# Products that nobody reads, put in front of TensorE's waits in a two-block transformer kernel

## What is computed

```python
def first_block(x, ...):                       # x: 1 x 256 x 1024
    for l in range(DEPTH):                     # DEPTH = 2
        x = x + 0.5 * swiglu_ffn(rms_norm(x, ffn1_norm[l]), ffn1_w_in[l], ffn1_w_out[l])
        h = rms_norm(x, mix_norm[l])
        uv, c_q, c_kv, k_rope, z, xbc, dt_raw, gates = jnp.split(h @ w_in[l], IN_OFFSETS, axis=-1)
        y_a, y_b, y_c = gmlp_mixer(...), mla_mixer(...), ssd_mixer(...)
        g = jax.nn.sigmoid(gates).reshape(bsz, s, 3, 1024)
        merged = (g[:, :, 0] * (y_a @ w_branch[l, 0]) + g[:, :, 1] * (y_b @ w_branch[l, 1])
                  + g[:, :, 2] * (y_c @ w_branch[l, 2]))
        x = x + merged @ w_out[l]
        x = x + 0.5 * swiglu_ffn(rms_norm(x, ffn2_norm[l]), ffn2_w_in[l], ffn2_w_out[l])
    return x

def second_block(x, mem, ...):                 # one layer
    h = x + _mixer(_rmsnorm(x, norm_mix_g), ...)          # gated delta rule and S5
    h = h + _cross_attn(_rmsnorm(h, norm_x_g), mem, ...)
    h = h + _swiglu(_rmsnorm(h, norm_ffn_g), w_gate, w_up, w_down)
    return _rmsnorm(h, norm_final_g)
```

## Time and profile before

| | |
|---|---|
| median of three runs | 1987.09 us |
| the three runs | 1983.67, 1988.60, 1987.09 us |
| the profiled execution, device time | 1975.48 us |
| its span, first to last instruction | 1973.8 us |
| mean clock granted to TensorE in it | 0.976 of full |
| PE busy | 1875.1 us, 95% of the span |

### The profile page before, as it was taken

How to read it: one execution, slowest core, us unless ns; L and a number is a source line. 1 busy time by engine, 2 the same in 40 slices (tenths; PEclk the granted TensorE clock), 3 DMA queues, 4 the chain that set the end, 5 groups by cost and what they waited for, 6 DMA issues and landing times.

```text
span 1973.8 us, 25367 instructions
## 1 busy us (share of the span) xinstructions
PE 1875.1 (95%) x10644; PEld 1535.2 (78%) x10644; DVE 934.4 (47%) x1166; ACT 709.9 (36%) x813; POOL 77.9 (4%) x145
## 2 busy tenths in 40 slices
PE   7999999997999999999999978999899999889998
PEld 7998575576899789985755667998787975749996
DVE  4544134467555444441335574545667431234453
ACT  5543213143454345441131343554223121214542
POOL 0000000000000000000000002000361100000000
PEclk9999999998999989999999999999998899989999
DMA  6545434343653565454344437736344223326353
GB/s 235 173 140 191 150 119 152 128 134 106 208 171 128 192 212 172 141 192 140 130 132 133 134 117 121 240 120 212 131 150 115 65 78 131 112 85 213 128 180 129
DMA packets 192244, 293.02 MB, mean 148 GB/s; under 512 B 7218, under 2 KB 126804, under 8 KB 192164
## 3 DMA queue, kind: packets, MB, share of 16 engines
q1 hardware_dynamic: 189908, 287.72, 43.4%
q0 software_dynamic: 1936, 4.14, 2.0%
q10 hardware_dynamic: 320, 0.01, 0.0%
HBM read 289.49 MB, written 2.36 MB: 148 GB/s over the span
## 4 chain that ended last, share of the span: by engine, by line
PE 90%; DVE 4%; DMA 2%; ACT 2%; issue 1%; DVEq 0%; SPq 0%; ACTq 0%
PE acc L221 17%; PE acc L223 17%; PE acc L222 17%; PE acc L189 16%; PE acc L253 7%; PE acc L409 2%; PE acc L2374 1%; PE acc L203 1%; PE acc L2682 1%; PE turn L308 1%; DMA ring<-in_ffn_w_out 1%; DMA ring<-in_ffn_w_in 1%; DVE w_lo L381 1%; PE acc L1161 1%; ACT w_hi L377 1%
## 5 line engine op out<-in xcount | busy, mean ns | idle before, releaser
L381 DVE TENSOR_TENSOR w_lo<-ring,w_hi 128x2048 fp32r<-128x2048 f32 x160 | 362.9, 2290 | 273.1 <-ACT w_hi L377 272.6
L221 PE MATMUL acc<-xT_hi,w_hi 128*128 128x256 f32 x1680 | 477.1, 284 | 3.0 <-DVE w_lo L381 3.0
L223 PE MATMUL acc<-xT_hi,w_lo 128*128 128x256 f32 x1680 | 476.2, 283 | 2.4 <-issue 2.4
L222 PE MATMUL acc<-xT_lo,w_hi 128*128 128x256 f32 x1680 | 476.1, 283 | 0.0
L377 ACT ACTIVATE w_hi<-ring 128x2048 fp32r<-128x2048 f32 x160 | 302.1, 1913 | 221.2 <-DMA ring<-in_ffn_w_out 110.3
L221 PEld LDWEIGHTS acc<-xT_hi,w_hi 128*128 128x128 f32 x1680 | 323.3, 192 | 5.9 <-issue 5.8
L222 PEld LDWEIGHTS acc<-xT_lo,w_hi 128*128 128x128 f32 x1680 | 323.2, 192 | 0.1
L223 PEld LDWEIGHTS acc<-xT_hi,w_lo 128*128 128x128 f32 x1680 | 323.2, 192 | 0.0
L189 PE MATMUL acc<-ring,xT 128*128 128x512 f32 (+2 forms) x736 | 303.2, 571 | 0.8 <-DVE xT L2662 0.8
L189 PEld LDWEIGHTS acc<-ring,xT 128*128 128x128 f32 x736 | 140.2, 192 | 153.9 <-issue 141.3
L221 PE MATMUL acc<-w_hi,hT_hi 128*128 128x512 f32 x440 | 173.0, 393 | 4.7 <-DVE w_lo L381 4.7
(11 more groups left out here) (503 smaller groups left out, 1984.2 us busy)
## 6 DMA issues: line engine op xcount, KB each, us to landing
ring<-in_ffn_w_in SPq DMA_DIRECT2D x88, 1024.0 KB, 5.5
ring<-in_w_in SPq DMA_DIRECT2D x48, 1024.0 KB, 5.1
ring<-in_ffn_w_out SPq DMA_DIRECT2D x44, 1024.0 KB, 4.9
ring<-in_w_branch SPq DMA_DIRECT2D x12, 1024.0 KB, 5.0
ring<-in_w_out SPq DMA_DIRECT2D x12, 1024.0 KB, 5.0
ring<-in_w_gate SPq DMA_DIRECT2D x11, 1024.0 KB, 5.2
ring<-in_w_up SPq DMA_DIRECT2D x11, 1024.0 KB, 7.1
ring<-in_w_down SPq DMA_DIRECT2D x11, 1024.0 KB, 4.9
```

What stands on the lines that cost most here:

```text
L221: pe.matmul(o, a_hi, wh, start=start, stop=False)
L222: pe.matmul(o, a_hi, wl, start=False, stop=False)
L223: return pe.matmul(o, a_lo, wh, start=False, stop=stop)
L381: vec.tensor_tensor(w_part(w_lo, r), raw_part(c0, r), w_part(w_hi, r).bitcast(F32), ALU.subtract).then_inc(f.lo, 1)
```

## The change

A new helper `keep_busy(pe, o, n)` issues n products of the identity with `causal`, 256 columns in float32, into the accumulator `o`. Each starts anew in the accumulator, counts no semaphore and waits for none, and nothing reads its result; the next real product into the accumulator starts anew as well. 127 of them are issued, in 24 places: 18 at the program's beginning, 7 or 5 in front of each turning of a norm that has a wait, 4 in front of each `first_gate`, and in both mixers of the first block 5 behind `G_KV`, 2 in front of the values, 6 in front of the last branch, 5 in front of the merged turning and 6 in front of `w_out`; in cross attention 5 and 2. In two places a wait is moved or added so that the accumulator is free: `wait_acc_free` stands ahead of the 4 products of `first_gate`, and `qs_pv_pe` first waits for `qs.vec` at 50 rather than 52.

```diff
--- before.py
+++ after.py
@@ -300,7 +300,13 @@
                                       gain.unsqueeze(2).broadcast_to([P, KD, P])[:, 4 * hf:4 * hf + 4, :],
                                       ALU.mult).then_inc(s.vec, 1)
 
-        def norm_pe(pe, s, nb=xn, tiles=(0, 1)):
+        def keep_busy(pe, o, n):
+
+            for _ in range(n):
+                pe.matmul(o[:, 0:TOK], ident[:, :], causal[:, :], start=True, stop=True)
+
+        def norm_pe(pe, s, nb=xn, tiles=(0, 1), busy=0):
+            keep_busy(pe, turn[2 * tiles[0]], busy)
             for b in range(2 * tiles[0], 2 * tiles[-1] + 2):
                 m, hf = b // 2, b % 2
                 pe.wait_ge(s.vec, s.tile(m))
@@ -401,9 +407,10 @@
             def first_gate():
 
 
+                wait_acc_free(pe, G0, 0)
+                keep_busy(pe, acc[bank(G0, 0)], 4)
                 pe.wait_ge(n.vec, n.v0 + 8)
                 wait_chunk(pe, c0)
-                wait_acc_free(pe, G0, 0)
                 for ft in range(2):
                     for k in range(KD):
                         ins = pe.matmul(acc[bank(G0, 0)][:, ft * TOK:(ft + 1) * TOK],
@@ -1304,6 +1311,8 @@
                     vec.tensor_copy(dst, turn[r % 4][:, :].rearrange("p (h n) -> p h n", h=4)).then_inc(qs.vec, 1)
 
             def qs_pv_pe(pe):
+                pe.wait_ge(qs.vec, 50)
+                keep_busy(pe, turn[2], 2)
                 pe.wait_ge(qs.vec, 52)
                 for m in range(MT):
                     for h in range(H):
@@ -1329,6 +1338,8 @@
 
             def branch_pe(pe, j):
                 b = BRANCHES[j]
+                if j == 2:
+                    keep_busy(pe, turn[0], 6)
                 pe.wait_ge(tail.vec, 2 + j)
                 for n in range(2):
                     split_group_pe(pe, tail, G_BR + 2 * j + n, C_BR + 2 * j + n, 2 + 2 * j + n, yT_hi[:, b], yT_lo[:, b],
@@ -1357,6 +1368,7 @@
                         vec.tensor_tensor(dst, dst, br_t[:, n, m, :], ALU.add).then_inc(br.vec, 1)
 
             def merged_pe(pe):
+                keep_busy(pe, turn[0], 5)
                 pe.wait_ge(br.vec, 8)
                 for b in range(4):
                     m, hf = b // 2, b % 2
@@ -1426,6 +1438,7 @@
                 group_pe(pe, G_CQ, C_CQ, xT, (4, 4), QR)
                 gm_mix_pe(pe)
                 group_pe(pe, G_KV, C_KV, xT, (4, 4), KVR + ROPE)
+                keep_busy(pe, turn[2], 5)
                 turned_group_pe(pe, G_XBC0, C_XBC0, xT, 4, 512)
                 cq_pe(pe)
                 gm_turn_pe(pe)
@@ -1454,6 +1467,8 @@
                 qs_pv_pe(pe)
                 branch_pe(pe, 2)
                 merged_pe(pe)
+                wait_acc_free(pe, G_WO, 0)
+                keep_busy(pe, acc[bank(G_WO, 0)], 6)
                 pe.wait_ge(tail.vec, 8)
                 for n in range(2):
                     split_group_pe(pe, tail, G_WO + n, C_WO + 2 * n, 8 + 2 * n, xT_hi, xT_rest, part_hi, part_lo, 2,
@@ -1566,12 +1581,12 @@
                 add_norm_vec(vec, ffn_add(C_FFN2, G_FFN2, 0.5, 3 * l + 3), n_next, gain0[:, 8 * l + 8:8 * l + 16])
 
             def pe_program(pe):
-                norm_pe(pe, n1, tiles=(1,) if l > 0 else (0, 1))
+                norm_pe(pe, n1, tiles=(1,) if l > 0 else (0, 1), busy=7 if l > 0 else 18)
                 if l == 0:
                     first_gain_pe(pe)
                 ffn_pe(pe, f1, n1, C_FFN1, G_FFN1, lambda e: norm_pe(e, mix_norm, tiles=(0,)), asides={7: params_pe})
                 mixer_pe(pe)
-                norm_pe(pe, n2)
+                norm_pe(pe, n2, busy=5)
                 ffn_pe(pe, f2, n2, C_FFN2, G_FFN2, lambda e: norm_pe(e, n_next, tiles=(0,)), asides={4: params2_pe, 6: s5_c_pe} if l == DEPTH - 1 else {})
 
             def sync_program(sync):
@@ -2707,7 +2722,7 @@
                 for product, which in itertools.islice(beside, n):
                     product(pe, *which)
 
-            norm_pe(pe, nm, tiles=(1,))
+            norm_pe(pe, nm, tiles=(1,), busy=7)
             pe.wait_ge(nm.vec, nm.v0 + NORM_DONE)
             turned_group_pe(pe, G_K2, C_K2, xT, 4, 512)
             turned_group_pe(pe, G_Q2, C_Q2, xT, 4, 512)
@@ -2741,17 +2756,19 @@
             pe.wait_ge(rc.vec, RC_DONE)
             group_pe(pe, G_WO2, C_WO2, xT, (4, 4), 512)
             group_pe(pe, G_WO2 + 1, C_WO2 + 2, xT, (4, 4), 512, for_x=True)
-            norm_pe(pe, nx)
+            norm_pe(pe, nx, busy=5)
             pe.wait_ge(nx.vec, nx.v0 + NORM_DONE)
             turned_group_pe(pe, G_XQ, C_XQ, xT, 4, 512)
             turned_group_pe(pe, G_XQ + 1, C_XQ + 2, xT, 4, 512)
             xa_scores_pe(pe)
+            keep_busy(pe, acc[0], 5)
             xa_turn_pe(pe)
+            keep_busy(pe, acc[0], 2)
             xa_pv_pe(pe)
             pe.wait_ge(xa.vec, 18)
             group_pe(pe, G_XO, C_XO, xT, (4, 4), 512)
             group_pe(pe, G_XO + 1, C_XO + 2, xT, (4, 4), 512, for_x=True)
-            norm_pe(pe, n3)
+            norm_pe(pe, n3, busy=5)
             ffn_pe(pe, f3, n3, C_FFN3, G_FFN3, lambda e: None)
 
         def second_act(act):
```

## The result

The changed kernel takes **1964.09 us** (median of four runs, 1960.97 to 1966.40); the kernel before took 1986.19 beside it. The ratio is 0.9888, 95% interval 0.9867 to 0.9909: faster by 22 us, 1.1%. The forecast was 1960 in a range of 1950 to 1975.

A forecast was written before the change was run, and what follows sets the result against it. PE bounds the kernel, with 90% of the chain and half clock behind its waits. Terms -18.0 + 2.1 + 0.1 + 0.5 = -15.3 us, from the profiled 1975.48, gave 1960 us; range 1950 to 1975.

The forecast's parts named there:

- The mechanism: At PE's waits: new products keep PE busy, so the clock does not fall there; 18.0 us taken away.
- `w_out`: Stretches at `w_out` in two layers: half-clock loss taken away, 2.8 us in the first and 1.5 in the second.
- `n1`: Norm `n1` of the second layer: 2.9 us of clock loss and 0.7 of slow turning taken away, first gate 0.79 late.
- the attention: Attention: 1.7 us of clock loss at the values and 0.7 of slow turning taken away, 0.1 of cost.
- Late first gates: 4 products before each first gate outlast the wait: 0.43 us at `n2` (twice) and `n3`, 0.79 at `n1`, together 2.1.
- The beginning: 18 products at the start end at about 11.9 us, 1.9 late; turnings then take 1.4 less; net cost 0.5 us.
- the choice of the base: Whole kernel: sum taken from the profiled 1975.48 us, without adding back the 11.6 us to the median of 1987.09.
- a loss of up to 7 us: Second block's small products, 14 us at a clock of 0.51: not touched by the change, they keep this loss.
- Partial hold: Rival, at the norms: new products hold the clock only in part; 1970 to 1982 us, say 1972; chance 0.18.
- Products that don't count: Rival, all filled places: new products are no activity for the clock; 16 us slower, 2003 us; chance 0.06.
- Gain given back: Rival: PE is earlier, but low weight halves or the ring of chunks end the next waits; 1980 to 1987 us; chance 0.06.
- Turnings: Between new products at norms: turnings count as activity for the clock, against the Trainium skill; no size of its own.

The follow-up runs named there:

- Thin products: Changed kernel with new products of 8 columns in place of 256, and twice as many: 1997.81 us, ratio 1.0072 to the kernel before.
- parts alone: Two cut-down changed kernels: new products only at norms and first gates, 1973.15 us; only in the first block's two mixers, 1981.36 us.
- e3: Changed kernel without the 4 new products in front of each first gate: 1967.35 us, ratio 0.9921 to the kernel before.
- e7: Changed kernel without the 18 new products at the program's beginning: 1962.22 us, ratio 0.9883 to the kernel before.
- e2: Changed kernel with twice as many new products in each place, 127 more: 1998.61 us, ratio 1.0082 to the kernel before.
- e4: Changed kernel with fewer new products at beginning and first gates, dt products put between wide ones, new products at open places such as S5: 1948.85 us, ratio 0.9830.

## Why the prediction was right, and where it was off

- **The mechanism and the terms hold.** For the filled places the sum said -15.3 us, and the two traces have -14.9. `w_out` 2.8 and 1.5 against 2.7 and 1.3; `n1` 2.9 + 0.7 - 0.8 against 3.0; `nm` 3.0 against 2.9; the attention 2.3 against 2.0; `n3` 2.0 against 2.0. Thin products and parts alone show the cause: the same places return to half clock when the products are thin or missing.
- **Late first gates** were priced at 2.1 us. At `n2` and `n1` the gate is 0.26 and 0.6 us late and not 0.43 and 0.79. By e3 they also prevent falls behind `n1`, a gain that the prediction did not name.
- **The beginning** was said to end at 11.9 with 4 us at half clock. The products took 10.9 us; 36 records at 0.216 are 7.8, so some 6 us were at half, and the turning began at 12.93. Net -0.6 where -1.2 stood, and e7 shows that without them the gate would have been as fast.
- **The step that failed is the choice of the base**: that the 11.6 us between the profiled execution and the median would all vanish, since "all should gather near the sum". They vanished by 6.8 (22.1 - 15.3). The falls move about in the places that the change leaves open too: the S5 stretch was at half clock for 13.7 us in both profiles of the kernel before, and for 23.9 and 13.7 us in the two of the changed kernel. The prediction gave these products a loss of up to 7 us; 23.9 us at half clock are 12. With 13.7 us the changed kernel took 1960.92 us, on the forecast; with 23.9 us 1966.40, and of the 5.5 us between these two executions 4.8 arose among the S5 products. The forecast of 1960 was thus the time of a lucky execution, and the median is 4 us above it. That the other executions of the changed kernel differ by the same stretch is likely and not shown: they have no trace.
- **The rivals.** Partial hold: no, every filled place was at 1.00 in both profiles. Products that don't count: excluded for wide ones, made real by thin ones. The argument against it can be made stronger: three quarters of `causal` are zeros, not half as the prediction has it, and the products held the clock. Gain given back: this was dismissed with "there was no such wait where the clock was full", but the trace of before has PE waiting for `w_lo` for 7.7 us in 6 waits, a row that the prediction did not look at. The longest of them took 3.9 us back, and 1.8 us were lost there in all; right behind the other first gates no such wait appeared.
- **Turnings.** The trace of before had spoken against the sentence of the Trainium skill (TensorE: Matmul & The Clock Gate, Part 4: PE-mode transpose) that full clock "doesn't engage" in transpose mode. The beginning of the same trace speaks against it too (16 turnings, then three records at full clock), and the norms stayed at 1.00 with the new products around them. No run here holds the clock with turnings alone.

## What to carry to other kernels

In this kernel a wait of 2 to 4 us cost TensorE twice: once itself, and again in the real products behind it at half clock (3 to 10 us of them). So look at the granted clock right behind PE's waits and not only at the waits. Products that nobody reads cost nothing where they fitted into the wait, and most of their length beyond it (29 to 38 of 55 us in e2); measure the wait at full clock, since a slow turning hides part of it. Where narrow products follow each other, look at the clock even if PE is 100% busy: here it fell among products of 8, 32 and 64 columns. Wide products of real work between them (dt in e4) or unread ones (S5 in e4) brought it back to full.

## What was not expected of the hardware

- The granted clock falls with hardly a wait. In the thin kernel it fell at 486.9 us behind 4 us in which PE had no gap over 0.55 us, and the 32- and 64-column products in the second block held half clock for up to 23.9 us with PE busy throughout. In the same places it was at 1.00 with new products of 256 columns and at half with products of 8.
- The profile's clock says 1.00 in the first us of the program, where 16 turnings took 3.65 us as at half clock. There, durations tell the clock, and the row does not:

```profile
10.00:14.00 4.00, 3.88 (x17) 3.43 (x17) 0.99 (x3) 0.17 (x1) 0.00 (x0) 1.00 1.09 387
```

- Executions of one kernel differ by where the clock falls: 1975.48 and 1980.22 us in two profiles of the same program, 1980 to 1992 us in the runs beside the experiments.
